# Second-layer projections as seven block products, with weight sums on VectorE and GpSimd

## The reference, cut to what matters

```python
def nsa_attention(x, w_in, w_out, pos_k, pos_v, ck_w1, ck_w2, cv_w1, cv_w2, rel_bias):
    proj = x @ w_in            # 256x1024 @ 1024x2608
    sizes = [H * d] + [Hkv * d] * 6 + [3 * H]
    q, kc, vc, ks, vs, kw, vw, g = jnp.split(proj, np.cumsum(sizes)[:-1].tolist(), axis=-1)
    ...
    kcmp = compress(kc, pos_k, ck_w1, ck_w2)   # blk = t[:, cidx] + pos; gelu(blk @ w1) @ w2
    vcmp = compress(vc, pos_v, cv_w1, cv_w2)
```

## Time and profile before

| | |
|---|---|
| runs | 1207.51 us median of 3 (1205.47 to 1207.91) |
| span of the profiled execution | 1202.5 us; its own time outside the span is not listed |
| TensorE matmul / weight load | 1017.6 us (85%) / 562.6 us (47%) |
| VectorE / ScalarE / GpSimd | 310.7 (26%) / 183.4 (15%) / 43.1 (4%) |
| DMA | 449.05 MB, mean 373 GB/s |
| mean granted TensorE clock | 0.931 of full speed |

### The profile page before, as it was taken

The page is one execution under the profiler, slowest core; times in us unless marked ns, Lnnn a source line. Parts: engine busy times, 40 slices in busy tenths (PEclk is TensorE's granted clock), DMA queues, the critical chain, the costliest instruction groups (busy, mean ns, idle before and its releaser), DMA issues.

```text
span 1202.5 us, 18281 instructions
## 1 busy us (share of the span) xinstructions
PE 1017.6 (85%) x7608; PEld 562.6 (47%) x7608; DVE 310.7 (26%) x867; ACT 183.4 (15%) x473; POOL 43.1 (4%) x109
## 2 busy tenths in 40 slices
PE   9999999976688966678899999999956788866775
PEld 7576544443342533244678655545523433423432
DVE  2435521321111111111212785403211111111112
ACT  1024210110010000000221562201100010100002
POOL 1001010000000000000100120100000000000000
PEclk9999999997899987788999999999997899977888
DMA  9936899999999999999992608999999999999995
GB/s 353 366 140 262 322 396 414 427 427 426 427 427 428 427 426 427 428 428 421 371 362 83 266 11 325 384 413 422 426 428 426 427 427 427 428 427 427 427 428 227
DMA packets 59347, 449.05 MB, mean 373 GB/s; under 512 B 4579, under 2 KB 10980, under 8 KB 32636
## 3 DMA queue, kind: packets, MB, share of 16 engines
q1 hardware_dynamic: 57248, 442.52, 89.6%
q0 software_dynamic: 1680, 4.88, 1.1%
q10 hardware_dynamic: 332, 0.42, 0.1%
HBM read 446.72 MB, written 1.07 MB: 372 GB/s over the span
## 4 chain that ended last, share of the span: by engine, by line
PE 52%; DMA 42%; DVE 3%; ACT 1%; issue 1%; SPq 1%; DVEq 0%
DMA ring<-in_moe_w_up 16%; PE bank L1036 15%; DMA ring<-in_moe_w_down 11%; DMA ring<-in_moe_w_gate 10%; PE bank L811 7%; DMA bias<-in_moe_w_up 5%; PE bank L889 5%; PE bank L1000 4%; PE bank L1118 3%; PE bank L1094 2%; PE bank L1272 2%; PE bank L1133 2%; PE bank L1381 1%; PE bank L1369 1%; PE bank L1105 1%; PE bank L1298 1%
## 5 line engine op out<-in xcount | busy, mean ns | idle before, releaser
L1036 PE MATMUL bank<-ring,work 128*32 128x256 f32 (+1 forms) x2656 | 327.2, 480 | 113.9 <-DMA ring<-in_moe_w_up 37.6
L1036 PEld LDWEIGHTS bank<-ring,work 128*32 128x32 f32 (+1 forms) x2656 | 151.6, 133 | 246.6 <-issue 216.8
L1682 DVE TENSOR_TENSOR work<-work,bank 128x256 f32<-128x256 f32 (+1 forms) x32 | 15.6, 488 | 512.2 <-PE bank L1036 512.2
L1118 PE MATMUL bank<-ring,work 128*32 128x512 f32 x576 | 92.0, 623 | 10.8 <-DMA ring<-in_moe_w_down 5.5
L811 PE MATMUL bank<-xT,ring 128*128 128x256 f32 x384 | 85.7, 382 | 0.0
L1036 PE MATMUL bank<-softmax_area,work 128*32 128x256 f32 (+1 forms) x352 | 63.4, 484 | 25.7 <-DMA ring<-in_moe_w_gate 18.9
L1695 DVE TENSOR_TENSOR xs<-xs,bank 128x512 f32<-128x512 f32 x112 | 71.2, 683 | 47.8 <-PE bank L1136 29.6
L1036 PE MATMUL bank<-bias,work 128*32 128x256 f32 (+1 forms) x384 | 79.0, 499 | 0.0
L811 PEld LDWEIGHTS bank<-xT,ring 128*128 128x128 f32 x384 | 72.1, 190 | 12.2 <-issue 2.7
L1000 PE MATMUL bank<-work,acc 128*128 128x128 f32 (+1 forms) x448 | 75.5, 323 | 0.0
L1000 PEld LDWEIGHTS bank<-work,acc 128*128 128x128 f32 x448 | 66.0, 191 | 16.6 <-issue 11.5
(11 more groups left out here) (287 smaller groups left out, 1121.3 us busy)
## 6 DMA issues: line engine op xcount, KB each, us to landing
ring<-in_moe_w_gate SPq DMA_DIRECT2D x44, 2048.0 KB, 29.5
ring<-in_moe_w_up SPq DMA_DIRECT2D x40, 2048.0 KB, 28.8
ring<-in_moe_w_down SPq DMA_DIRECT2D x36, 2048.0 KB, 29.1
softmax_area<-in_moe_w_down SPq DMA_DIRECT2D x8, 2048.0 KB, 25.9
ring<-in_moe_w_down SPq DMA_DIRECT2D x12, 1024.0 KB, 8.2
ring<-in_moe_w_gate SPq DMA_DIRECT2D x12, 1024.0 KB, 9.2
bias<-in_moe_w_gate SPq DMA_DIRECT2D x6, 2048.0 KB, 33.7
softmax_area<-in_moe_w_up SPq DMA_DIRECT2D x6, 2048.0 KB, 28.5
```

The lines of the kernel that those rows point to most:

```text
L1036: last = mm(bank[2 + k][row:row + cap, 0:width], xgT_of(group_of[i])[:, t, at + e * cap:at + (e + 1) * cap], w[e](t)[:, part * width:(part ...
L1118: last = mm(bank[5][row:row + CAP_NARROW, :], hidT_narrow[:, m, CAP_NARROW * e:CAP_NARROW * (e + 1)], w[e](m)[:, n * 512:(n + 1) * 512], s ...
```

## The change: seven block products for kv, qa and qb

Each of the three slots W (1024 x 512) and the activations X are cut in 2 x 2 blocks: depths in halves of 512, columns in halves of 256, tokens in halves of 128. Four sums of X blocks (`s1` to `s4`, once for the layer) and four sums of W blocks (`t1` to `t4`, one of them in place, for each slot) let seven block products stand for eight. Each product has 8 matmuls of 128x128 weights by 128 tokens, so 16 records. Seven additions of 128 x 512 elements for each slot put the results together on VectorE, after one scaled copy on ScalarE.

- kv's weight sums are on VectorE (`sum_w_blocks`), qa's and qb's on GpSimd (`sum_query_weights`). GpSimd starts qb only after kv's last product, since both use the same area for sums.
- Result banks are shared in a fixed rotation (`unit_banks`). TensorE waits for the last reader of a bank before it writes the next product there (`result_read`).
- The first products of qa come before the gate columns, which move to bank 4. qa's other products stand around the gate tokens, qb's around the transposes of the hidden rows. TensorE waits for qb's last addition before the second compression product.
- `copy_cmp_in` now reads kv from SBUF (`kv_rows`), not from PSUM.
- The slots are given free after each slot's seventh product.
- Some semaphores that existed once for each layer are now shared by both.

```diff
+        NSA_UNITS = {"kv": 1.0, "qa": DH ** -0.5, "qb": DH ** -0.5}
+        unit_banks.update({
+            "kv": {"p1": (0, None), "p2": (1, None), "p6": (5, None), "p7": (0, ("kv", "p1")), "p5": (1, ("kv", "p2")),
+                   "p3": (5, ("kv", "p6")), "p4": (0, ("kv", "p7"))},
+            "qa": {"p1": (2, None), "p2": (3, None), "p6": (2, ("qa", "p1")), "p7": (3, ("qa", "p2")), "p5": (1, ("kv", "p5")),
+                   "p3": (0, ("kv", "p4")), "p4": (3, ("qa", "p7"))},
+            "qb": {"p1": (5, ("kv", "p3")), "p2": (1, ("qa", "p5")), "p6": (0, ("qa", "p3")), "p7": (5, ("qb", "p1")),
+                   "p5": (1, ("qb", "p2")), "p3": (0, ("qb", "p6")), "p4": (5, ("qb", "p7"))}})
...
+            def sum_query_weights(u, n):                              # GpSimd
+                pool.wait_ge(loaded[slot_no(use)], loads_through(use))
+                nc.gpsimd.tensor_tensor(t3, b22, b12, ALU.subtract).then_inc(queries_summed, 1)
...
+                nc.gpsimd.tensor_tensor(b12, b12, b11, ALU.subtract).then_inc(queries_summed, 1)
...
+                nc.gpsimd.tensor_tensor(t2, b22, b12, ALU.subtract).then_inc(queries_summed, 1)
...
+                nc.gpsimd.tensor_tensor(t4, b21, t2, ALU.subtract).then_inc(queries_summed, 1)
...
                 if l:
                     nc.gpsimd.memset(cmp_in[:, :, :, KV * N_CMP:], 0.0).then_inc(pads_ready, 1)
+                    sum_query_weights("qa", 1)
+                    pool.wait_ge(product_done, products_through("kv", "p4"))
+                    sum_query_weights("qb", 2)
...
+            def unit_products(u, *names):                             # TensorE
+                for p in names:
+                    b, before = unit_banks[u][p]
+                    if before:
+                        result_read(*before)
+                    if p == "p6":
+                        pe.wait_ge(sums_by(u), sums_through(u, "t2"))
+                        pe.wait_ge(x_summed, X_SUMS_BEFORE[unit_layer[u]] + 2)
...
+                    elif p == "p4":
+                        pe.wait_ge(sums_by(u), sums_through(u, "t4"))
+                    w, x = unit_of[u][p]
+                    for n in range(2):
+                        for t in range(HALF_K):
+                            last = mm(bank[b][:, n * P:(n + 1) * P], w[:, t, n * P:(n + 1) * P], x[:, t, :],
+                                      start=(t == 0), stop=(t == HALF_K - 1))
+                    last.then_inc(product_done, 1)
...
-            first_tiles(0, 0)
+            pe.wait_ge(xT_copied, 2 * 2 * NT + 1)
+            unit_products("kv", "p1")
+            xT_here(2, 0)
+            unit_products("kv", "p2")
             normed(0, 1, 1)
             transpose_x(2, 1)
-            first_tiles(0, 1)
-            for g in range(2):
-                first_tiles(1, g).then_inc(proj_ready[1], 1)
+            arrived(1, 1)
+            unit_products("qa", "p1", "p2")
+            xT_here(2, 1)
             nsa_group(2)
+            unit_products("kv", "p6", "p7", "p5", "p3", "p4")
...
-            nsa_group(3)
+            unit_products("qa", "p6", "p7", "p5")
...
-            nsa_group(4)
+            unit_products("qa", "p3", "p4")
...
+            result_read("qa", "p6")
             pe.wait_ge(cin_ready, 1)
...
-            nsa_group(5)
+            arrived(1, 2)
+            unit_products("qb", "p1", "p2", "p6")
+            result_read("qa", "p4")
             pe.wait_ge(chid_ready, 1)
...
-            nsa_group(6)
+            unit_products("qb", "p7", "p5", "p3", "p4")
+            result_read("qb", "p4")
             pe.wait_ge(chidT_ready, 1)
...
+            weights_here(0)                                           # VectorE
+            sum_w_blocks("kv", "t3", "t1", "t2")
+            add_products("kv", "c11")
+            dve.wait_ge(xT_copied, 2 * 3 * NT)
+            sum_x_blocks(1, *nsa_x_sums)
+            add_products("qa", "c11")
+            sum_w_blocks("kv", "t4")
+            add_products("kv", "u2")
+            add_products("kv", "u3")
+            add_products("kv", "c22", "u4", "c12")
+            add_products("kv", "c21")
+            dve.wait_ge(product_added, adds_through("kv", "c21"))
+            link(copy_cmp_in(v.tensor_copy, 0, kv_rows[:, 0, :, :].rearrange("p n q -> p (n q)")))
+            add_products("qa", "u2", "u3")
             dve.wait_ge(cpos_ready, 1)
...
-            dve.wait_ge(proj_act[1], 1)
+            dve.wait_ge(cin_act, 1)
...
             last.then_inc(cin_ready, 1)
+            add_products("qa", "c22", "u4", "c12", "c21")
...
-            nsa_copy(4)
-            nsa_copy(6)
+            add_products("qb", "c11", "u2", "u3", "c22", "u4", "c12", "c21")
```

More of the change, by code:

```diff
@@ L351, in build, with count_of, sums_through, sums_by @@
         loaded = [sem(f"loaded{s}") for s in range(NSLOT + 5)]
+        def count_of(*order):
+            at = {what: n + 1 for n, what in enumerate((u, name) for u, names in order for name in names)}
+            return lambda u, name: at[u, name]
+        products_through = count_of(
+            ("kv", ("p1", "p2")),
+            ("qa", ("p1", "p2")),
+            ("kv", ("p6", "p7", "p5", "p3", "p4")),
+            ("qa", ("p6", "p7", "p5", "p3", "p4")),
+            ("qb", ("p1", "p2", "p6", "p7", "p5", "p3", "p4")))
+        copies_through = count_of(
+            ("kv", ("p1",)),
+            ("qa", ("p1",)),
+            ("qb", ("p1",)))
+        adds_through = count_of(
+            ("kv", ("c11",)),
+            ("qa", ("c11",)),
+            ("kv", ("u2", "u3", "c22", "u4", "c12", "c21")),
+            ("qa", ("u2", "u3", "c22", "u4", "c12", "c21")),
+            ("qb", ("c11", "u2", "u3", "c22", "u4", "c12", "c21")))
+        kv_sums_through = count_of(
+            ("kv", ("t3", "t1", "t2", "t4")))
+        query_sums_through = count_of(
+            ("qa", ("t3", "t1", "t2", "t4")),
+            ("qb", ("t3", "t1", "t2", "t4")))
+        def sums_through(u, name):
+            return (kv_sums_through if u == "kv" else query_sums_through)(u, name)
+        def sums_by(u):
+            return w_summed if u == "kv" else queries_summed
+        product_done, product_copied, product_added = sem("product_done"), sem("product_copied"), sem("product_added")
+        w_summed, queries_summed, x_summed = sem("w_summed"), sem("queries_summed"), sem("x_summed")
+        for u, n in (("kv", 0), ("qa", 1), ("qb", 2)):
+            unit_w[u] = slot8(ring_use["fixed", 1, n, 0])
+        unit_of.update({u: unit_operands(unit_w[u], unit_w_sums[u], nsa_x_sums) for u in ("kv", "qa", "qb")})
         x_loaded, first_loaded = [sem(f"x_loaded{tt}") for tt in range(NT)], [sem(f"first_loaded{k}") for k in range(2)]
@@ L488, in slot_for, with copy_cmp_in @@
             return slot_views[s].rearrange("p (t n) -> p t n", t=4 if kind == "down" else KT)
-        def copy_cmp_in(copy, b, ps):
-            for hkv in range(KV):
+        def copy_cmp_in(copy, b, ps, heads=range(KV)):
+            for hkv in heads:
                 for o in range(2):
@@ L1351, in nsa_group @@
                     return
[L1352 to L1355, removed]
-                    arrived(1, use)
[L1357 to L1363, removed]
-                else:
-                    if half or g == 8:
-                        proj_bank_free(1, g)
+                use = {7: 5, 8: 5, 9: 6, 10: 6}[g]
+                w = nsa_slot(slot8, use)
+                if g == 7:
+                    result_read("qb", "p5")
+                elif g == 8:
+                    result_read("qb", "p3")
+                elif g == 9:
+                    pe.wait_ge(proj_act[1], 1)
+                elif half:
+                    pe.wait_ge(proj_dve[1], 2)
+                if g % 2:
+                    arrived(1, use)
+                    last = project_T(1, g, w, [tile_cols(0), tile_cols(1)], free=True)
+                else:
                     for tt in ((0,) if half else (1,) if g == 10 else range(NT)):
```

225 lines of the change are left out of this document (151 added, 74 removed).

## The result

The changed kernel takes 1214.74 us (median of 4 runs, 1212.56 to 1218.03) against 1206.49 us for the kernel before (4 runs). The profiled execution was the fastest of the four: 1212.56 us, 1.8 over its span of 1210.8. The forecast was 1203.6, and the range ended at 1211.5.

A forecast was written before the change was run, and what follows sets the result against it. TensorE's work was taken to bound layer 1's projection stage: 4.65 us less work, less a 0.75 us new wait, gives 3.9 us, so span 1198.6 plus 5.0 makes 1203.6 us. The range was 1202.0 to 1211.5.

The forecast's parts named there:

- The stage: Layer 1's projections, 587.94 to 659.66: TensorE busy 71.72 of 71.72 us, so less work there means less time.
- the new wait at qb's end: TensorE waits for VectorE's last qb addition before L1425: 0.75 us new, hidden by no other work.
- TensorE's work: Seven products for eight in each slot: kv saves 1.85 us, two query slots 1.40 each, 4.65 in all.
- qa's load: Load of qa's weights lands at 592.0, TensorE asks for it at 592.45: 0.5 us to spare.
- T: Time of one GpSimd sum of 1024 elements: taken as 3 us; any value up to 5 gives the same forecast.
- the cover of the copies at the compression product: Compression input ready at 615.0, wanted at 616.55: cover shrinks from 11 us to 1.5.
- rival B: GpSimd and VectorE sums take turns at SBUF: loss 6 to 9 us against gain 3.9, about 1211; chance 0.24.
- its own formula: With turns taken at SBUF, s2 ends at 595.0 + 3T, not 596.0; kv p6 wants it at 597.9.
- 5.0 us for the time outside the span: Difference between span 1202.5 and median 1207.5, added to the new span of 1198.6.
- T = 1.9: GpSimd sum time, with a wait of 3.9 us, from which taking turns at SBUF was said to decide.

The follow-up runs named there:

- e1_vector: Changed kernel with all weight sums, both query slots' too, on VectorE and none on GpSimd; 1200.43 us, ratio 0.9963 to the kernel before.
- e3: Changed kernel with only qa's GpSimd sums started later, behind VectorE's sums of X blocks; ratio 1.0031 to the kernel before.
- e4: Changed kernel with only qb's GpSimd sums started later, behind the position adds; ratio 1.0014 to the kernel before.
- e6: e1_vector with TensorE's wait for qb's last addition moved behind the second compression product's first part; 1201.48 us, ratio 0.9963 to the kernel before.
- e2_apart: Changed kernel, all eight sums still on GpSimd, qa's started after VectorE's X sums, qb's after the position adds; 1201.65 us, ratio 0.9968 to the kernel before.

## Why the prediction was wrong

**Right.** The stage was TensorE's list of work and the gain or loss in it reached the end: stage differences of +7.51, -3.63, +3.66, +2.40 and -4.21 us (changed kernel, e1_vector, e3, e4, e6) stand beside ratios that are +9.5, -4.5, +3.7, +1.7 and -4.5 us of 1206. What makes up the 2 us by which the changed kernel's ratio exceeds its stage is not shown: only the fastest of its four executions has a trace. The total, and the new wait at qb's end, were right to 0.3 us once GpSimd is out of the way: forecast 3.9 us less, measured 3.63 in e1_vector and e2_apart. Two small misses partly offset each other in it: TensorE's work fell by 4.15 us (71.72 to 67.57), not 4.65, since a product takes 1.83 us and not 1.80 (38.4 for the 21 of e1_vector, by the starts), and the wait at qb's end is 0.52, not 0.75. GpSimd's sum takes 2.36 us alone, under the 5 that the schedule bears. qa's load landed in time (TensorE's first qa product has no wait).

**Wrong.** The step that failed is the one that gave VectorE's sums and the copy their durations from rows without GpSimd beside them, and held that any T up to 5 us gives the same time. With T = 2.36, s1 to s3 took 8.1 us in place of 2.1, t2 3.27 in place of 1.22, and the eight copies 11.00 in place of 3.3. The path failed with it: the prediction counted the cover of the copies at the compression product (1.5 us), but the wait came one product earlier. qa's p4 needs the bank that the addition u3 frees, and u3 stands behind the copies on VectorE. That made the two waits, 3.07 + 4.53 = 7.60 us, and the clock behind them 3.3 more by the record times (5.28 in place of 3.68, 3.18 in place of 1.88, 7.46 in place of 7.06, by the starts, against e1_vector): 10.9 of the 11.14 between e1_vector and the changed kernel.

This was rival B, at 0.24. Its mechanism is shown, but its loss of 6 to 9 us fell short of 11.14, although its first wait was put higher than it came (6.1 us at T = 3, or 4.2 at 2.36 by its own formula; measured 3.07). It fell short for two reasons. It let GpSimd's qb sums meet only the position adds; the copies, which had become SBUF to SBUF through this very change, were counted as free of it, and they cost most. And it had no term for the clock. The one overlap in the earlier trace rows weighed too much against B: 0.14 us of overlap with a 0.2 us instruction can't show a wait for a whole instruction.

The Trainium skill (SBUF — State Buffer, Who interferes with whom) has the rule as measured here: an instruction of VectorE with two SBUF inputs contends with one of GpSimd that reads SBUF, whoever starts first holds the port pair for the whole instruction, and the other waits. The trace of e2_apart agrees in both directions (1.22 to 3.27 us, 2.36 to 3.22). The same section of the Trainium skill names `copy` among the operations that can take the shared pair, if its operands meet certain conditions; the 11.00 and 7.86 us fit that. The prediction did not apply it when the copy's source moved from PSUM to SBUF. The other page of the Trainium skill cited there (GPSIMD Engine Reference, 3.1 Elementwise) gave an estimated 2.3 us for T, measured 2.36.

**Smaller.** The additions were taken as 512 elements at 0.7 us; a result block is 128 x 256, and they last 0.42. It made VectorE's chain shorter than forecast (0.52 us at qb's end, forecast 0.75) and decided nothing. The text on the change, ahead of the prediction, has the same slip where it says 128 x 512 of an addition.

The forecast adds 5.0 us for the time outside the span. Each of the changed kernel's four runs shows 1.8 (1212.56 against 1210.8 in the profiled one), so most of the 5.0 will have been the distance between a median and a profiled execution below it. The median of 1200.4 us in e1_vector is therefore 3 under the forecast of 1203.6, though the stage is 0.3 longer than forecast; in ratio to the kernel before the two agree (0.9968 and 0.9963). The threshold that the prediction gives for B, T = 1.9, does not follow from its formula either: 595.0 + 3T passes 597.9 by 3.9 us at T = 2.27.

Not settled: why the lower clock lasts about twice as long behind the same waits in e3_qa_later and e4_qb_later as in the changed kernel.

## What to carry to other kernels

Before moving work to an idle GpSimd, list what VectorE does at the same time by where each operand lies: with one operand in PSUM and at most one in SBUF (the additions and the copies out of PSUM here) nothing was lost; with two SBUF operands, or a copy from SBUF to SBUF, each instruction can wait for a whole one of GpSimd, so a cover must be counted in GpSimd instructions. Two semaphore waits that kept the sums off the sums of X blocks and off the copies turned 0.8% slower into 0.3% faster, with the same work on the same engines. Where a stage has no wait now, count for a new one of several us a stretch of slow TensorE clock as well: 1.6 to 2.9 us were lost to it behind each of the waits of 3.1 and 4.5 us here, nothing behind one of 1.4.

## What the runs showed that was not expected

- A copy of 64 x 240 elements from SBUF is no slower on VectorE than from PSUM (3.08 against 3.34 us for eight), although it steps over 16 elements, but on ScalarE it is: 4.95 us for eight against 2.97, in every variant of the change, with or without GpSimd.
- GpSimd's memset of 1024 elements takes 0.95 to 0.97 us and holds VectorE's copies from SBUF to SBUF back; the two-operand adds it did not touch in the one run that tried it.
- Dummy matmuls in a wait keep the clock at 1.00, but gave back 1.6 of 3.3 us, since the wait behind was set by VectorE.
